# Retention stage of a two-block transformer kernel: x's sums made while a factor is spread, scores scaled in place in PSUM, second root ahead of the keys, last head's gate tiles taken one by one

## The chip, the core and the metric

The kernel runs on one core of a Trainium2 chip. The metric is the device time of one execution in microseconds; the number compared is the median over several runs. Engines: PE (TensorE, matrix products; PEld is its weight load), DVE (VectorE), ACT (ScalarE), POOL (GpSimd), SP (SyncE, which here only issues DMAs). Each engine has its own instruction list, worked through in order; semaphores tie the lists together.

## What is computed

Two blocks over 512 positions of 1024 features, all in fp32. The first block is a convolution mixer and a gated FFN. The second has a retention layer, an MLP, a chunked attention layer and another MLP. The change touches the retention layer only:

```python
def _retention(h, w_in, gn_g, w_out):            # B=1, S=512, 4 heads, dk=256, dv=512, chunks of 64
    q, k, v, g = jnp.split(h @ w_in, [RET_QK, 2 * RET_QK, 2 * RET_QK + RET_VW], axis=-1)
    q = _rope(q, pos)                            # [t1*cos - t2*sin, t1*sin + t2*cos]
    k = _rope(k, pos) * (RET_DK ** -0.5)
    ...
    scores = einsum('bhid,bhjd->bhij', qb, kb) * intra_decay   # and a running state between chunks
    ...                                          # o: decayed (q k^T) v over all earlier chunks and the own one
    mu, var = mean(o), mean((o - mu)**2)         # per position and head
    o = ((o - mu) * rsqrt(var + EPS)) * gn_g
    return (silu(g) * o) @ w_out
```

Here `h = rmsnorm(x) * mix_norm_g`, and x itself is first normalised once more, since this layer sits behind the final norm of the first block. So two factors per position are needed: `rc` (both norms together) for the layer's input and `rc2` (the first norm alone) for the residual x.

## The kernel before

**Precision.** Every fp32 matrix is split into a high half (rounded to the PE's fp32r format) and a low half (the rest), and each product is three matmuls: high by high, low by high, high by low (`product`, lines 865 to 869). For weights, ACT makes the high half (L1420) and POOL the low half (L833), in halves of a block of 128 x 2048. For activations ACT makes the high half and DVE the low one.

**Units.** PE works in units of 24 products of 128 x 512 (three matmuls for each of 8 tiles, or 4 x 2). `unit_done` counts units that PE has ended, `unit_taken` those whose PSUM bank has been read. PSUM has 8 banks (`ps[:, 0..7]`); weights have two slots, so ACT converts the block after next once PE has let go of a slot (`after_unit` waits for a unit and then calls `convert`).

**Retention, its start.** PE runs four units of the first head's queries (units 0, 1, in banks 0, 1) and keys (units 2, 3, in banks 2, 3). Between them it sums the squares (`stats`, bank 4) and spreads the factor `rc` over the partitions by products of ones with `diagonals` (`spread`, L954, bank 5). DVE copies the spread factor to `r_bc` (L2491), multiplies it into the tables cos and sin (L2495) and rotates (`rope`, L2498): four products of a bank with a table into `sg` in SBUF (L2502 to L2505), a subtraction and an addition within `sg` (L2507, L2508). ACT makes the high half of the result (L1438) and DVE the low one (L2515).

**Retention, value and gate.** Each head has seven quarters of a Strassen-like scheme (`HEAD_QUARTERS`: h11, d1, h22, d2, d3, h21, d4), two units each. The quarters d1, h22, d2 and d3 multiply sums of x over tiles and positions. DVE makes these once, at the start (`position_sum`, L2544, four instructions per sum; `w` is an intermediate held in banks 6 and 7), ACT and DVE split them (L1776, L2552), and SP stores three of them in DRAM for the later heads (L637) and fetches them again (L610). The matching sums of weights are made by DMAs of POOL that add onto a loaded block (`add_to`, L785); p1 to p4 are those behind d1 to d4: p3, for instance, is issued when h22's low half is made, and d3 can be converted only when p3 has landed.

**Retention, one head.** Order on PE: h11; for head 0 a second `spread`, of `rc2`, for later heads the scores; d1, h22; for head 0 the scores; d2, d3, mix of tiles 0 and 1, h21, mix of tiles 2 and 3, d4, then (but for the last head) the next head's query units, the 16 transposes of the gated output (`head_turn`, L1204), the next key units, and four output units. h11 writes banks 0 and 1 and waits until the units there are taken; d1 writes banks 2 and 3 and waits until the keys are taken. Scores come in four tiles of 512, 384, 256 and 128 columns in banks 4 to 7. DVE multiplies each with the decay into `ptf` in SBUF (`score`, L2567), ACT makes the high half from `ptf` (L1438) and DVE the low half (`score_lo`, L2558). d3 waits for `value_sum` (L2585), which stands behind the four `score_lo` and two copies on DVE.

**End of a head.** `mixed_stats` gives the variance, ACT the root (`make_root`, L1429), DVE refines it (`refine_root`) into `t4`. The gate's four tiles come from h21 (0 and 1, `gate_sum`) and d4 (2 and 3, `gate_copy`, L2602). ACT applies silu (`gate_curve`, L1711) and then `t4` (`scale_gate`, L1718), DVE forms the gated output (`gated`, L2615), PE turns it. On ACT the order is: silu of 0 and 1, root, the conversions behind the two units of d4, silu of 2 and 3, the four scalings.

**Order.** Nothing is scheduled: each engine's order is the order of its code, and within `ret` that is `head` and the lines behind it.

## Time and profile before

| | us |
|---|---|
| median of 3 runs (lowest, highest) | 1893.45 (1893.13, 1895.30) |
| the profiled execution, its own time | 1893.47 |
| its span, first to last instruction | 1891.5 |
| PE busy in it | 1831.4 (97%) |
| DVE, POOL, ACT busy | 1191.0, 1021.6, 884.3 |
| mean granted TensorE clock | 0.989 |
| retention stage in it | about 536 to 976 |

The profile is of one execution. Times in its rows run from the start of the span. "Idle before" is an engine's time without work ahead of an instruction, put down to the wait that ended last. PE is busy nearly all the time, so the kernel's time changes where PE waits, where its clock is low, or where its work changes.

### The profile page before, as it was taken

How to read it: one execution, taken by the hardware profiler on the slowest of the kernel's cores; microseconds unless marked ns; L12 is line 12 of the kernel's file. 1: busy time of each engine (PE TensorE's matmuls, PEld its weight loads, DVE VectorE, ACT ScalarE, POOL GpSimd, SP SyncE). 2: the span in 40 equal slices, each digit the busy share in tenths (PEclk: the TensorE clock that was granted, in tenths of full speed). 3: DMA queues.
4: the chain of work that ended last, by engine and by line, in shares of the span. 5: the costliest groups of instructions: out<-in, count | busy, mean ns of one | idle time of the engine just before them, and what ended most of it. 6: DMA issues, size and time to landing. Idle time of an engine off the chain costs nothing.

```text
span 1891.5 us, 23910 instructions
## 1 busy us (share of the span) xinstructions
PE 1831.4 (97%) x9348; PEld 1557.3 (82%) x9348; DVE 1191.0 (63%) x1859; ACT 884.3 (47%) x1370; POOL 1021.6 (54%) x447
## 2 busy tenths in 40 slices
PE   9999999999986999999799999999999999999998
PEld 7778889898874888878689898988888887888886
DVE  6986875775776564545466354457877766454546
ACT  5345443342443535252545444455566646353444
POOL 5573465475536456565537575664233336664755
PEclk9999999999998999999899999999999999999999
DMA  5222424432257547473442332312433222414221
GB/s 184 90 89 70 154 67 145 148 108 93 87 178 192 169 115 225 112 208 90 124 156 88 113 112 68 134 45 66 122 111 110 81 79 98 156 53 147 91 89 56
DMA packets 150705, 218.61 MB, mean 116 GB/s; under 512 B 4513, under 2 KB 94897, under 8 KB 150081
## 3 DMA queue, kind: packets, MB, share of 16 engines
q1 hardware_dynamic: 134880, 187.97, 29.9%
q0 software_dynamic: 8448, 16.78, 5.1%
q10 hardware_dynamic: 7264, 12.34, 2.2%
q8 instruction: 74, 1.21, 0.3%
q14 instruction: 39, 0.31, 0.0%
HBM read 207.59 MB, written 9.48 MB: 115 GB/s over the span
## 4 chain that ended last, share of the span: by engine, by line
PE 73%; DVE 10%; ACT 4%; POOL 4%; issue 2%; DMA 2%; ACTq 0%; DVEq 0%
PE ps L867 24%; PE ps L868 23%; PE ps L869 23%; POOL w_lo L833 4%; DMA work<-in_ret_w_in_dram 2%; ACT w_hi L1420 1%; DVE ps L2344 1%; DVE diagonals L2012 1%; PE ps L1204 0%; DVE xl L2038 0%; DVE probs_t_lo L2558 0%; ACT work L1892 0%; DVE probs_t_lo L2787 0%; PE ps L1294 0%; DVE work L2781 0%
## 5 line engine op out<-in xcount | busy, mean ns | idle before, releaser
L833 POOL TENSOR_TENSOR w_lo<-raw,w_hi 128x1024 fp32r<-128x1024 f32 x220 | 532.6, 2430 | 615.1 <-ACT w_hi L1420 615.1
L867 PE MATMUL ps<-xh,w_hi 128*128 128x512 f32 x1280 | 504.2, 394 | 5.1 <-DVE xl L2038 3.0
L869 PE MATMUL ps<-xh,w_lo 128*128 128x512 f32 x1280 | 498.5, 389 | 0.0
L868 PE MATMUL ps<-xl,w_hi 128*128 128x512 f32 x1280 | 498.3, 389 | 0.0
L1420 ACT ACTIVATE w_hi<-raw 128x1024 fp32r<-128x1024 f32 x238 | 247.6, 1057 | 385.1 <-PE ps L869 342.7
L867 PEld LDWEIGHTS ps<-xh,w_hi 128*128 128x128 f32 x1280 | 240.3, 188 | 59.8 <-issue 8.2
L868 PEld LDWEIGHTS ps<-xl,w_hi 128*128 128x128 f32 x1280 | 240.4, 188 | 50.3 <-issue 1.9
L869 PEld LDWEIGHTS ps<-xh,w_lo 128*128 128x128 f32 x1280 | 240.3, 188 | 50.4
L867 PE MATMUL ps<-hid,w_hi 128*128 128x256 f32 (+1 forms) x688 | 228.9, 333 | 2.2 <-DVE att_v L2741 0.9
L868 PE MATMUL ps<-hid,w_hi 128*128 128x256 f32 (+1 forms) x688 | 227.3, 330 | 0.0
L869 PE MATMUL ps<-hid,w_lo 128*128 128x256 f32 (+1 forms) x688 | 227.3, 330 | 0.0
L833 POOL TENSOR_TENSOR w_lo<-work,w_hi 128x1024 fp32r<-128x1024 f32 x60 | 145.3, 2463 | 41.6 <-ACT w_hi L1420 41.6
L867 PEld LDWEIGHTS ps<-hid,w_hi 128*128 128x128 f32 x688 | 131.1, 191 | 15.6 <-issue 2.3
L833 POOL TENSOR_TENSOR w_lo<-down,w_hi 128x1024 fp32r<-128x1024 f32 x40 | 96.2, 2420 | 83.9 <-ACT w_hi L1420 83.8
L869 PEld LDWEIGHTS ps<-hid,w_lo 128*128 128x128 f32 x688 | 130.9, 190 | 12.2
L868 PEld LDWEIGHTS ps<-hid,w_hi 128*128 128x128 f32 x688 | 131.1, 191 | 11.7 <-issue 0.2
L867 PE MATMUL ps<-w_hi,hid 128*128 128x512 f32 x224 | 90.7, 405 | 18.3 <-DVE ps L2585 12.0
L2253 DVE TENSOR_TENSOR x<-x,ps 128x512 f32<-128x512 f32 x84 | 56.9, 684 | 74.8 <-PE ps L869 74.7
L1420 ACT ACTIVATE w_hi<-work 128x1024 fp32r<-128x1024 f32 x60 | 62.0, 1056 | 85.2 <-PE ps L869 43.8
L2702 DVE SCALAR_TENSOR_TENSOR work<-ps,r_bc 128x512 f32<-128x512 f32 x64 | 43.6, 690 | 79.6 <-PE ps L869 79.5
L833 POOL TENSOR_TENSOR w_lo<-holder,w_hi 128x1024 fp32r<-128x1024 f32 x24 | 57.7, 2420 | 59.4 <-ACT w_hi L1420 59.4
L868 PE MATMUL ps<-w_lo,hid 128*128 128x512 f32 x224 | 88.6, 395 | 0.0
(292 smaller groups left out, 3523.1 us busy)
## 6 DMA issues: line engine op xcount, KB each, us to landing
raw<-in_mlp_w_dram SPq DMA_DIRECT2D x40, 1024.0 KB, 5.5
work<-in_mlp_w_dram SPq DMA_DIRECT2D x16, 1024.0 KB, 5.9
raw<-in_ret_w_in_dram SPq DMA_DIRECT2D x12, 1024.0 KB, 5.4
raw<-in_att_w_in_dram SPq DMA_DIRECT2D x12, 1024.0 KB, 5.3
raw<-in_w_gate_dram SPq DMA_DIRECT2D x11, 1024.0 KB, 5.3
raw<-in_w_up_dram SPq DMA_DIRECT2D x11, 1024.0 KB, 5.4
raw<-in_w_in_dram SPq DMA_DIRECT2D x9, 1024.0 KB, 5.1
down<-in_mlp_w_dram SPq DMA_DIRECT2D x8, 1024.0 KB, 5.7
```

What stands on the lines that cost most here:

```text
L833: nc.gpsimd.tensor_tensor(half_of(wl[:, b % 2, :], b, half), half_of(source, b, half), half_of(wh[:, b % 2, :], b, half).bitcast(F32), ALU ...
L867: nc.tensor.matmul(o, a[0], b[0], start=first, stop=False, skip_group_check=True)
L868: nc.tensor.matmul(o, a[0], b[1], start=False, stop=False, skip_group_check=True)
L869: return nc.tensor.matmul(o, a[1], b[0], start=False, stop=last, skip_group_check=True)
L1420: nc.scalar.activation(half_of(wh[:, b % 2, :], b, half), source, ACT.Copy).then_inc(w_hi, c.made(w_hi))
L2012: V.reciprocal(rough, root_rows).then_inc(dve_step, c.made(dve_step))
L2253: V.tensor_tensor(tiles, tiles, ps[:, where, :].rearrange("p (m c) -> p m c", m=2), ALU.add).then_inc(unit_taken, c.made(unit_taken))
L2344: V.scalar_tensor_tensor(total if last else acc, src, w, acc, ALU.mult, ALU.add).then_inc(signal, c.made(signal))
L2702: V.scalar_tensor_tensor(hval[:, u % 2, :], bank(), 0.0, r_bc[:, :], ALU.max, ALU.mult).then_inc(unit_taken, c.made(unit_taken))
```

## The change

Four edits of the retention stage, plus one in SP's queue that goes with them. The number of matmuls does not change.

1. At the start, DVE makes the sums `w` and `d2` between writing the diagonals and reading the spread factor, then takes the factor, rotates the queries, and makes `d1`. ACT converts h11's weights ahead of the halves of the sums, not behind them. `rope` is split: its two products with cos are written in place in PSUM, the subtraction and addition read PSUM and write `sg`, and only the last of these six instructions releases the banks (it was the fourth). The low half is `rope_lo`.
2. The second root is asked for behind d2's low half, `rc2`'s diagonals stand ahead of the rotation of the keys, and the sum `d3` and its halves behind it. PE's scores wait for all four sums' low halves.
3. `score` multiplies in place in PSUM, and both halves are made from there.
4. At the end of a head the root stands between silu of tile 0 and of tile 1. In the last head the scalings of tiles 0, 1, 2 stand ahead of silu of tile 3, and the two conversions of weights behind all of them.
5. SP fetches the next head's query weights right ahead of its key weights, behind d3's conversion; they were fetched behind h11's.

```diff
@@ SP, per head
-                        if more:
-                            converted("h11", h)
-                            fetch("q", h + 1)
                         multiplied("d1", h)
...
                         if more:
                             converted("d3", h)
+                            fetch("q", h + 1)
                             fetch("k", h + 1)
@@ PE, head_scores
                         pe.wait_ge(qk_ready, c.next(qk_ready, 2))
+                        pe.wait_ge(sum_lo, len(SUM_ROW))
@@ ACT
-                            hi_of(pth[:, cut], ptf[:, cut])
+                            hi_of(pth[:, BY_KEY[j]:BY_KEY[j] + n], ps[:, 4 + j, 0:n])
...
                         gate_curve(h, 0)
+                        make_root()
                         gate_curve(h, 1)
-                        make_root()
...
+                        else:
+                            unit_ended()
+                            gate_curve(h, 2)
+                            scale_gate(h, (0, 1, 2))
+                            unit_ended()
+                            gate_curve(h, 3)
+                            scale_gate(h, (3,))
+                            convert(2)
                         turned_hi(h)
...
                     make_root()
                     scale_far(4)
+                    after_unit()
+                    after_unit()
+                    rotated_hi(qh, "q", 0)
                     position_sum_hi("d1")
                     position_sum_hi("d2")
-                    qk_hi_of(qh)
+                    after_unit()
+                    after_unit()
+                    make_root()
                     position_sum_hi("h22")
                     act.wait_ge(sum_lo, SUM_ROW["d2"] + 1)
                     scale_far(0)
+                    rotated_hi(kh, "k", 0)
                     position_sum_hi("d3")
-                    make_root()
-                    qk_hi_of(kh)
@@ DVE
+                    def rope(bank):
...
                         V.tensor_tensor(sg[:, 1, :], a, sin, ALU.mult)
+                        V.tensor_tensor(sg[:, 0, :], b, sin, ALU.mult)
+                        V.tensor_tensor(a, a, cos, ALU.mult)
+                        V.tensor_tensor(b, b, cos, ALU.mult)
+                        V.tensor_tensor(sg[:, 0, :], a, sg[:, 0, :], ALU.subtract)
+                        V.tensor_tensor(sg[:, 1, :], b, sg[:, 1, :], ALU.add).then_inc(unit_taken, c.made(unit_taken, 2))
...
-                        V.tensor_tensor(ptl[:, cut], ptf[:, cut], pth[:, cut].bitcast(F32), ALU.subtract)
+                        V.tensor_tensor(ptl[:, cut], ps[:, 4 + j, 0:SEQ - P * j], pth[:, cut].bitcast(F32), ALU.subtract)
...
-                        V.tensor_tensor(ptf[:, cut], ps[:, 4 + j, 0:n], decay[:, h % 2, 0:n], ALU.mult)
+                        V.tensor_tensor(ps[:, 4 + j, 0:n], ps[:, 4 + j, 0:n], decay[:, h % 2, 0:n], ALU.mult)
```

Two places show how the lists move. The first is DVE's list at the start of the stage, from the second factor's root to the first query or key rotation behind it. `cols` are the small per-position columns, `diagonals` the matrix that PE spreads, `hid` the halves of a sum, `work` the SBUF area of tables, `sg` and sums. Before:

```order
L2691 COPY cols<-cols 128x4
L2523 RECIPROCAL ps<-cols 128x4 [waits curve_made]
L2525 TENSOR_TENSOR cols<-ps,cols 128x4 [waits dve_step]
L2527 SCALAR_TENSOR_TENSOR cols<-ps,cols 128x4 [waits dve_step]
L2529 SCALAR_TENSOR_TENSOR cols<-cols,ps 128x4 [waits dve_step]
L2002 TENSOR_TENSOR diagonals<-ident,cols 128x512 [waits root_refined]
L2502 TENSOR_TENSOR work<-ps,work 128x512 [waits unit_done]
L2503 TENSOR_TENSOR work<-ps,work 128x512
L2504 TENSOR_TENSOR work<-ps,work 128x512
L2505 TENSOR_TENSOR work<-ps,work 128x512
L2507 TENSOR_TENSOR work<-work 128x512 [waits unit_taken]
L2508 TENSOR_TENSOR work<-work 128x512
```

The same place after the change:

```order
L2531 RECIPROCAL ps<-cols 128x4 [waits curve_made]
L2533 TENSOR_TENSOR cols<-ps,cols 128x4 [waits dve_step]
L2535 SCALAR_TENSOR_TENSOR cols<-ps,cols 128x4 [waits dve_step]
L2537 SCALAR_TENSOR_TENSOR cols<-cols,ps 128x4 [waits dve_step]
L2019 TENSOR_TENSOR diagonals<-ident,cols 128x512 [waits root_refined]
L2560 TENSOR_TENSOR hid<-work,hid 128x1024 [waits sum_made,sum_hi]
L2512 TENSOR_TENSOR work<-ps,work 128x512 [waits unit_done]
L2513 TENSOR_TENSOR work<-ps,work 128x512
L2514 TENSOR_TENSOR ps<-ps,work 128x512
L2515 TENSOR_TENSOR ps<-ps,work 128x512
L2517 TENSOR_TENSOR work<-ps,work 128x512 [waits dve_step]
L2518 TENSOR_TENSOR work<-ps,work 128x512
```

The sum h22's low half has moved between the diagonals and the rotation of the keys, and the rotation's last two instructions now read PSUM. Before the change, all four sums stood ahead of these rows; after it, `d3`, its four instructions and its two halves, stands behind them.

The second is ACT's list at the end of the last head. `w_hi<-holder` are the conversions of output weights, `cols<-cols` is the root. Before:

```order
L1711 ACTIVATE work<-work,cols 128x512 [waits unit_taken] x2
L1429 ACT_TABLE_LOAD
L1429 ACTIVATE cols<-cols 128x4 [waits to_curve]
L1420 ACTIVATE w_hi<-holder 128x8x128 [waits holder_landed2,unit_done]
L1420 ACTIVATE w_hi<-holder 128x8x128 [waits holder_landed2]
L1711 ACT_TABLE_LOAD
L1711 ACTIVATE work<-work,cols 128x512 [waits unit_taken] x2
L1718 ACTIVATE work<-work,cols 128x512 [waits gate_made,root_refined]
L1718 ACTIVATE work<-work,cols 128x512 [waits gate_made] x3
L1723 ACTIVATE hid<-ps,prm 128x512 [waits turned] x4
```

The same place after the change:

```order
L1712 ACTIVATE work<-work,cols 128x512 [waits unit_taken]
L1431 ACT_TABLE_LOAD
L1431 ACTIVATE cols<-cols 128x4 [waits to_curve]
L1712 ACT_TABLE_LOAD
L1712 ACTIVATE work<-work,cols 128x512 [waits unit_taken]
L1712 ACTIVATE work<-work,cols 128x512 [waits unit_taken,unit_done]
L1719 ACTIVATE work<-work,cols 128x512 [waits gate_made,root_refined]
L1719 ACTIVATE work<-work,cols 128x512 [waits gate_made] x2
L1712 ACTIVATE work<-work,cols 128x512 [waits unit_taken,unit_done]
L1719 ACTIVATE work<-work,cols 128x512 [waits gate_made,root_refined]
L1419 ACTIVATE w_hi<-holder 128x8x128 [waits holder_landed2] x2
L1724 ACTIVATE hid<-ps,prm 128x512 [waits turned] x4
```

The number of table loads is the same; the conversions have moved from ahead of the last two silus to behind the last scaling.

## Rows read from the trace of the kernel before

**Rows 1.** Who waited for whom, PE, 536 to 976: total us, times, longest.

```profile
PE ps L867 <- DVE ps L2585: 12.0, 3, 9.4
```

**Rows 2.** PE in order of time at the stage's start: start, us, idle before.

```profile
562.26 0.79 PE L867 MATMUL ps<-w_hi,xh 128*128 128x512 f32 x1 [4.91 <-DVE work L2505]
...
577.80 2.08 PE L954 MATMUL ps<-diagonals,ones 128*128 128x128 f32 x8 [7.83 <-DVE diagonals L2002]
580.19 0.80 PE L867 MATMUL ps<-w_hi,hid 128*128 128x512 f32 x1 [0.32 <-DVE work L2505]
...
613.58 0.79 PE L867 MATMUL ps<-w_hi,hid 128*128 128x512 f32 x1 [9.37 <-DVE ps L2585]
```

**Rows 3.** Busy time by stretch: us, five engines with instruction counts, PE clock, DMA share, GB/s.

```profile
928.00:942.00 14.00, 5.45 (x22) 4.79 (x21) 6.62 (x9) 9.82 (x13) 4.65 (x2) 0.63 0.00 0
```

**Rows 4.** Chain that ended last, at the third gap's end: start, us, what.

```profile
616.93 0.43 PE ps L868
...
618.03 0.23 PE ps L868
```

**Rows 5.** DVE in order of time at the stage's start.

```profile
549.94 1.29 DVE L2495 TENSOR_TENSOR work<-work,r_bc 128x512 f32<-128x512 f32 x2
551.27 3.36 DVE L2544 SCALAR_TENSOR_TENSOR ps<-x,prm,ps 128x256 f32<-128x256 f32 x8
...
557.45 1.23 DVE L2552 TENSOR_TENSOR hid<-work,hid 128x1024 fp32r<-128x1024 f32 x1 [1.13 <-ACT hid L1776]
...
561.52 0.68 DVE L2505 TENSOR_TENSOR work<-ps,work 128x512 f32<-128x512 f32 x1
562.24 2.35 DVE L2507 TENSOR_TENSOR work<-work 128x512 f32<-128x512 f32 x1
...
602.48 8.99 DVE L2558 TENSOR_TENSOR probs_t_lo<-work,probs_t_hi 128x512 fp32r<-128x512 f32 x4 [3.57 <-ACT probs_t_hi L1438]
```

**Rows 6.** POOL in order of time, the same stretch.

```profile
559.37 4.67 POOL L833 TENSOR_TENSOR w_lo<-raw,w_hi 128x1024 fp32r<-128x1024 f32 x2 [18.33 <-ACT w_hi L1420]
...
590.67 1.30 POOL L785 DMA_DIRECT2D work<-in_ret_w_in_dram  x1 [0.30 <-POOL w_lo L833]
...
601.07 5.16 POOL L833 TENSOR_TENSOR w_lo<-work,w_hi 128x1024 fp32r<-128x1024 f32 x2 [2.30 <-ACT w_hi L1420]
```

**Rows 7.** ACT in order of time, the same stretch.

```profile
599.92 2.01 ACT L1420 ACTIVATE w_hi<-work 128x1024 fp32r<-128x1024 f32 x2 [6.63 <-DMA work<-in_ret_w_in_dram]
601.84 1.53 ACT L1438 ACTIVATE probs_t_hi<-work 128x512 fp32r<-128x512 f32 x4
```

**Rows 8.** ACT in order of time at the end of the last head.

```profile
928.48 2.00 ACT L1420 ACTIVATE w_hi<-holder 128x1024 fp32r<-128x1024 f32 x2 [2.15 <-PE ps L869]
...
931.80 1.33 ACT L1711 ACTIVATE work<-work,cols 128x512 f32<-128x512 f32 x2
933.04 2.54 ACT L1718 ACTIVATE work<-work,cols 128x512 f32<-128x512 f32 x4
```

**Rows 9.** DVE, the same stretch.

```profile
933.77 3.03 DVE L2615 SCALAR_TENSOR_TENSOR work<-work,cols 128x512 f32<-128x512 f32 x4 [4.65 <-ACT work L1718]
```

**Rows 10.** PE, the same stretch.

```profile
936.95 3.65 PE L1204 MATMUL ps<-ident,work 128*128 128x128 f32 x16 [8.55 <-DVE work L2615]
940.25 0.78 PE L867 MATMUL ps<-hid,w_hi 128*128 128x512 f32 x1
```

**Rows 11.** Chain that ended last, heads 0 to 3.

```profile
842.45 1.75 PE ps L1204 x16
...
889.51 10.77 DMA work<-in_ret_w_in_dram
```

**Rows 12.** SP's issues in order of time, head 1.

```profile
712.90 0.37 SPq L606 DMA_DIRECT2D work<-in_ret_w_in_dram  x1
```

**Rows 13.** ACT in order of time, head 1.

```profile
724.88 2.01 ACT L1420 ACTIVATE w_hi<-raw 128x1024 fp32r<-128x1024 f32 x2 [4.34 <-PE ps L869]
```

**Rows 14.** DMA issues of the whole run: KB each, median us to landing.

```profile
raw<-in_ret_w_in_dram SPq DMA_DIRECT2D x12, 1024.0 KB, 5.4
```

## What the change should do to the time

> **What bounds the kernel now.** I read the page's busy times first, then the list of who waited for whom on PE in the retention stage, then the three engines in order of time around each of PE's gaps. PE is busy 97% of the span, so the question is where it is not. In 536 to 976 us nearly all its idle time lies in four gaps. Three are at the start of the stage: 4.91 us ahead of h11, 7.83 ahead of the second spread, 9.37 ahead of d3 [rows 2]. One is ahead of the last head's transposes, 8.55 [rows 10]. The waits of the kind that end ahead of d3 sum to 12.0 in three heads, so 2.6 are left for heads 2 and 3 [rows 1]. Each big gap costs more than itself. Behind the third, matmuls start 0.43 us apart and later 0.23 apart [rows 4], that is at 1.2 and then at 2.4 GHz, and the stretch 928 to 942 has a mean clock of 0.63 [rows 3]. From the rows I put the slow matmuls behind the first gap at 2.0 us of loss (ten at 0.2), behind the second at 3.4 with the spread's 2.08 where about 0.9 is its due, behind the third at 1.9. With small gaps of 0.3 to 0.7 each around d1 and h22, PE loses about 31 us between the end of the key units (557.35 = 562.26 - 4.91) and d3. The check: h11, spread, d1, h22, scores and d2 at full clock are 4 x 5.45 + 0.9 + 3.75 = 26.5 us (24 products at 0.227, scores 10 tiles of products by width), so d3 could start at 583.8; it starts at 613.58 and then still loses the 1.9.
>
> Why DVE is late there: an instruction with both inputs in SBUF stands still while POOL works. L2507 takes 2.35 where POOL's pair runs from 559.37 for 4.67, and the four-instruction group L2558 takes 8.99 beside POOL's 5.16 and the pair behind it; L2505, which reads PSUM during the same POOL pair as L2507, takes 0.68 [rows 5, 6].
>
> **The change, step by step.** All times are my estimates on the profile's clock, built from its durations. A DVE instruction of 512 columns goes at 0.6 to 0.7 us, a sum's four at 0.42 each (3.36 for eight), a half of 1024 columns 1.23, on ACT 1.06 [rows 5].
>
> *First gap.* `w` and `d2` now lie under the wait for the spread (diagonals end 545.2, spread ends 549.2; the sums' 3.36 fit). Factor copy, tables 1.29, then the rotation. ACT converts h11 at about 545.4, so POOL's 4.67 lie over the tables, two-SBUF instructions: their cost is 1.29 (POOL idle) to 3.6 (a stall like L2507's); I take 2.7, since POOL's pair would end near 551.2. The rotation runs 552.6 to 556.4, six instructions now before the banks are free where four did. That is before PE ends the keys at 557.35. Gap 4.91 becomes 0 and the clock stays up: h11 runs 557.4 to 562.8.
>
> *Second gap.* DVE: d1 to 558.1, q's low half to 559.4, d1's and d2's low halves to 561.8, sum h22 to 563.7, root refined 564.5, then the diagonals. POOL is at d1's weights then (ACT converts them 560.2 to 562.1 behind d2's high half; POOL 561.3 to 566.0). The diagonals read ident and columns, both in SBUF. Cost 0.69 to 2.35, the same two rows as bounds; I take the upper one, since the rotation's subtraction is the same form beside the same POOL work, so they are done at 566.8. PE idles 4.0 us. The spread needs about 1 us, but d1 waits for the keys' banks: h22's low half to 568.1, rotation 3.75, so 571.9. The old wait was released by the fourth instruction; the two more cost 1.3 us here. PE idles 3 us more, the clock is low as behind the other gaps of this kind, and I charge 1.9 + 1.2. d1 ends at 579.3 (before: near 587.4).
>
> The Trainium skill, page "SBUF — State Buffer", section "SBUF: two separate sides", says that a two-SBUF-input VectorE instruction and a GpSimd one take a port pair as an exclusive lock and the loser blocks fully. It speaks for edit 3 and against the moved tables and diagonals: by it these stall 1.4 and 1.5 us; with the rows' lower bounds instead, d3 would start some 1.5 us earlier and the time be 1867.5.
>
> *Third gap.* DVE behind the rotation: d3 to 573.6, k's low half to 574.8, d3's to 576.1, factor copy and the kept products of h11. ACT reaches h22's conversion at 574.7, POOL ends it at 580.5, and h22 runs on PE 579.3 to 584.8 with no wait over 0.7. Scores end at 588.5, d2 at 594.0. The new bound is the transfer p3: POOL issues it behind h22's low half, at 580.8. Before, it was issued at 590.67 and ACT went on at 599.92 [rows 6, 7], 9.25 later; in head 3 the like transfer took 10.77 [rows 11]. The fetch of sum d3 (multiplied d1 at 579.3, stored by 581.5) now runs beside it as in head 3, so I take 10.3 and 591.1. ACT then converts d3, 2.0, and makes the scores' high halves, 1.53 [rows 7]. DVE's low halves follow each within 0.7 (PSUM input, no stall): 595.6. Two copies and `value_sum`, 2.0: d3 starts at 597.6. Gap 3.6 instead of 9.37. I take it without a clock loss, as its length is below all four that had one. Gain of the three together: 613.58 + 1.9 - 597.6 = **17.9**.
>
> *Last head.* The last unit ends at 928.4. Before: conversions 2.00, table load 1.3 (930.48 to 931.80), silus, scalings to 935.58, DVE to 936.8 [rows 8, 9]. Now ACT has silu of 0 at 924.2, table load, root 925.6, load 926.9, silus of 1 and 2 by 928.3, three scalings of 0.63 by 930.1, silu 930.8, last scaling 931.4. DVE's last of four follows at 932.2. PE starts turning 4.7 earlier. The conversions now lie in front of ACT's reading of the turned tiles: they end at 933.4, so the first product comes at 934.9 where it came at 940.25 [rows 10]. That is 5.35. If the clock stays up (3.8 us of idle) 0.8 more is saved on the first products: **6.1**. If it falls, the transposes take 3.65 and not 1.75 [rows 10, 11] and the gain is 4.6.
>
> *Heads 1 to 3.* PE waits only 2.6 + some 0.7s there [rows 1], for the chain through p3, which is bound by the transfer and not by DVE. I give it 0.4. The score halves' stalls vanish from DVE but no one waits for them. Root ahead of silu: nothing. The later release of the key banks lies under the first output unit, 5.45 long. The later fetch of the next queries goes out at 712.90 with the keys' [rows 12]; 1 MB lands 5.4 later [rows 14], ACT takes it at 724.88 [rows 13], so 6 us are in hand: nothing.
>
> *Sum.* 17.9 + 6.1 + 0.4 = 24.4 off the profiled execution's own 1893.47 gives 1869.1; the median shown is 1893.45, the same. I say 1869.
>
> **Rivals.**
> (A) *The new bound bites harder.* p3 lands 11.5 after issue, d3 starts 1.2 later, PE's gap is 4.8 and the clock falls as behind the 4.91 one (+2), and it falls in the last head too (+1.5): 1869.1 + 4.7 = 1874. For it: the 4.91 gap is the nearest, and two other gaps of mine are near 4. Against: the third needs two things at once.
> (B) *The stalls do not come.* Tables and diagonals find POOL between its instructions, p3 takes 9.25, the clock stays up ahead of d1: 1.5 + 1.0 + 1.9 less, 1865.
> (C) *The change doesn't do what it says.* Score halves from PSUM stall as those from SBUF did: 8.99 instead of 3, d3 6 us later and a slow clock behind, 1869.1 + 8 = 1877. Against: L2505's 0.68 beside POOL.
> (D) *Slower.* The next queries, now queued with the keys behind d3, come late in heads 0, 1, 2. ACT wants them 12 us after issue; with POOL's pair and PE ready near 735, PE itself is held only from 18.6 after issue. To eat 24.4 us it must be 8.1 late in each of three heads, landing 27 after issue; at 30 it is 3 x 11.4 - 24.4 = +9.8, 1903. Against: 5.4 median, no row near it.
>
> **How the numbers follow.** Forecast 0.52, A 0.19, B 0.15, C 0.10, D 0.02, the rest (0.02) anything else near no change. The forecast's own spread is the bounds used: tables and diagonals, transfer 9.25 to 11.5, the last head's clock: about 1866.5 to 1871.5. To hold 8 in 10 the range takes in A and most of B: 1864 to 1875.5. What a measurement of this kernel tells from no change is about 0.2%, 3.8 us. Faster 0.96, same 0.02, slower 0.02.
>
> **What would show each step.** PE without a gap ahead of h11; spread near 567 and d1 near 572; L2507's successor at 0.7 and not 2.3; tables near 2.7; p3's landing as releaser of d3's conversion and value_sum ahead of d3 near 597.6; score low halves at 0.3 to 0.7 each; transposes near 932 on the old clock with PE's clock still full. I would be wrong if PE had a new gap in the middle of head 0, or ahead of the first output units, where turned tiles now wait for ACT's conversions.

## The result, and the profile after

The changed kernel took 1877.5 us (median of four executions, 1875.3 to 1877.67), the kernel before 1893.44 beside it: a ratio of 0.9911 with a 95% interval of 0.9894 to 0.9928. The forecast was 1869 with a range of 1864 to 1875.5. So the sign and most of the steps came out, and the size did not: 16 us were gained of 24.4. Four more executions of the same kernel, run later beside the experiments, gave 1873.75, 1873.82, 1875.37 and 1878.16. The eight have a median of 1876.4. The profiled execution of after is the one of 1877.67, its span 1875.7.

I count gains as the start of the same matmul in the profile of before minus its start in that of after. The first view is PE in order of time, start and duration in us and the idle time ahead; it answers [rows 2].

```profile
566.33 2.07 PE L952 MATMUL ps<-diagonals,ones 128*128 128x128 f32 x8 [3.75 <-DVE diagonals L2019]
571.19 0.79 PE L865 MATMUL ps<-w_hi,hid 128*128 128x512 f32 x1 [2.79 <-DVE work L2518]
```
```profile
598.91 0.80 PE L865 MATMUL ps<-w_hi,hid 128*128 128x512 f32 x1 [5.15 <-DVE ps L2592]
599.50 0.63 PE L866 MATMUL ps<-w_lo,hid 128*128 128x512 f32 x1
...
602.86 0.39 PE L865 MATMUL ps<-w_hi,hid 128*128 128x512 f32 x1
```

There is no gap ahead of h11 any more. The spread starts 11.5 us earlier, d1 9.0, d3 14.7 (613.58 - 598.91). The gap of 5.15 ahead of d3 is what is left of 9.37, and the matmuls behind it still take 0.63 until 602.5.

The list of who waited for whom on PE, 536 to 976, in total us, times and the longest, answers [rows 1]:

```profile
PE ps L865 <- DVE ps L2592: 8.7, 4, 5.1
PE ps L1203 <- DVE work L2622: 4.9, 2, 4.2
PE ps L952 <- DVE diagonals L2019: 3.8, 1, 3.8
PE ps L865 <- DVE work L2518: 2.8, 1, 2.8
```

DVE in order of time in the prologue answers [rows 5]. The tables took 2.74. The low halves of the scores take 1.69 from PSUM where they took 8.99 from SBUF. The copy of four columns in the middle is new to this list, and so are the diagonals' 0.69 behind it:

```profile
549.73 2.74 DVE L2699 TENSOR_TENSOR work<-work,r_bc 128x512 f32<-128x512 f32 x2
...
561.34 1.97 DVE L2706 COPY cols<-cols 128x4 f32<-128x4 f32 x1
...
565.58 0.69 DVE L2019 TENSOR_TENSOR diagonals<-ident,cols 128x512 f32<-128x512 f32 x1
...
595.11 1.69 DVE L2566 TENSOR_TENSOR probs_t_lo<-ps,probs_t_hi 128x512 fp32r<-128x512 f32 x4 [6.64 <-ACT probs_t_hi L1440]
```

POOL's issue of the transfer p3 and of p4, SP's fetch of the sum for d3, and ACT's conversion of d3 that p3 releases, each from its own engine's list in order of time. They answer [rows 6, 7]:

```profile
579.86 1.30 POOL L783 DMA_DIRECT2D work<-in_ret_w_in_dram  x1 [0.30 <-POOL w_lo L831]
...
586.22 1.29 POOL L783 DMA_DIRECT2D holder<-in_ret_w_in_dram  x1 [0.30 <-POOL w_lo L831]
```
```profile
579.96 0.58 SPq L610 DMA_DIRECT2D hid<-position_sums  x1
```
```profile
592.59 2.01 ACT L1419 ACTIVATE w_hi<-work 128x1024 fp32r<-128x1024 f32 x2 [12.55 <-DMA work<-in_ret_w_in_dram]
594.50 1.40 ACT L1440 ACTIVATE probs_t_hi<-ps 128x512 fp32r<-128x512 f32 x4
```

The end of the last head on ACT and PE answers [rows 8, 10]. The order is as forecast, and PE's idle time is 4.17 instead of 8.55, but the 16 transposes still take 3.05, where they took 1.75 in head 2 [rows 11]:

```profile
915.29 1.93 ACT L1719 ACTIVATE work<-work,cols 128x512 f32<-128x512 f32 x3
917.12 0.70 ACT L1712 ACTIVATE work<-work,cols 128x512 f32<-128x512 f32 x1
917.92 0.72 ACT L1719 ACTIVATE work<-work,cols 128x512 f32<-128x512 f32 x1
918.55 1.99 ACT L1419 ACTIVATE w_hi<-holder 128x1024 fp32r<-128x1024 f32 x2
```
```profile
919.57 3.05 PE L1203 MATMUL ps<-ident,work 128*128 128x128 f32 x16 [4.17 <-DVE work L2622]
922.27 0.78 PE L865 MATMUL ps<-hid,w_hi 128*128 128x512 f32 x1
```

Followed along the whole program, the gain is 14.7 at d3 of head 0, 13.0 when the last head's last unit ends, 18.1 behind that head's end, 15.7 behind 1320 us of the changed kernel, and 15.8 at the end. The drop of 2.4 lies in the attention layer, where the change touches nothing. The questions were therefore: why d3 is 1.3 us later than forecast and slow behind; what is lost in heads 0 and 1; whether the last head's clock is PE's standing still; and what the 2.4 are.

### The profile page after: what moved, and what is told of

Its sections match the earlier page's. It is cut to its first block, busy times and chain, and to the rows that moved or that the text cites. A ratio compares the mean times of both kernels' runs of the same rounds, so it can differ in the third digit from the quotient of the medians.

```text
span 1875.7 us, 23906 instructions
## 1 busy us (share of the span) xinstructions
PE 1830.6 (98%) x9348; PEld 1557.2 (83%) x9348; DVE 1168.3 (62%) x1859; ACT 883.9 (47%) x1370; POOL 1019.2 (54%) x447
## 4 chain that ended last, share of the span: by engine, by line
PE 72%; DVE 10%; ACT 4%; POOL 4%; DMA 2%; issue 2%; ACTq 0%; DVEq 0%
PE ps L865 23%; PE ps L867 23%; PE ps L866 23%; POOL w_lo L831 4%; DMA work<-in_ret_w_in_dram 2%; ACT w_hi L1419 1%; DVE ps L2361 1%; DVE diagonals L2029 1%; DVE probs_t_lo L2810 0%; PE ps L1203 0%; DVE xl L2055 0%; DVE work L2804 0%; ACT work L1909 0%; PE ps L1293 0%; DVE work L2622 0%
## 5 line engine op out<-in xcount | busy, mean ns | idle before, releaser
L865 PE MATMUL ps<-w_hi,hid 128*128 128x512 f32 x224 | 90.5, 404 | 15.9 <-DVE ps L2592 8.7
L867 PE MATMUL ps<-w_hi,hid 128*128 128x512 f32 x224 | 88.6, 396 | 0.0
```

The lines of the kernel that those rows point to most:

```text
L865: nc.tensor.matmul(o, a[0], b[0], start=first, stop=False, skip_group_check=True)
L867: return nc.tensor.matmul(o, a[1], b[0], start=False, stop=last, skip_group_check=True)
```

## The experiments

All times stand beside runs of the kernel before on the same chip; its medians in the five groups were 1893.83 (e1 to e4), 1892.97 (e5 to e8), 1893.93 (e9 to e11, the changed kernel again), 1894.28 (e12 to e14) and 1894.15 (e15 to e17). Variants of the changed kernel whose medians are one or two us apart mostly have overlapping intervals of their ratios. There a reading rests on the traces at the place of the edit, one trace for each kernel, and not on the medians.

### One part alone

**The scores alone.** The kernel before, with part 3 of the change only.

```diff
-                            hi_of(pth[:, cut], ptf[:, cut])
+                            hi_of(pth[:, BY_KEY[j]:BY_KEY[j] + n], ps[:, 4 + j, 0:n])
...
-                        V.tensor_tensor(ptl[:, cut], ptf[:, cut], pth[:, cut].bitcast(F32), ALU.subtract)
+                        V.tensor_tensor(ptl[:, cut], ps[:, 4 + j, 0:SEQ - P * j], pth[:, cut].bitcast(F32), ALU.subtract)
...
-                        V.tensor_tensor(ptf[:, cut], ps[:, 4 + j, 0:n], decay[:, h % 2, 0:n], ALU.mult)
+                        V.tensor_tensor(ps[:, 4 + j, 0:n], ps[:, 4 + j, 0:n], decay[:, h % 2, 0:n], ALU.mult)
```

> The kernel before with one edit of the change alone: scores scaled in place in PSUM, the high and low halves read from there. In the kernel before the four low halves took 8.99 us (602.48 to 611.5) beside POOL; from PSUM they took 1.69 in the changed kernel. Theory (the SBUF read is what stalls, and in the kernel before it stands alone behind the transfer p3): the low halves end near 604.9, two copies and value_sum follow, d3 starts near 607 where it was 613.58, and with the gap of 9.37 down to about 3 the clock may stay up: 6.5 to 8.4 us saved, 1885 to 1887. Rival (something else, such as POOL's low half of d3's weights, sets d3's start): under 3 us saved, above 1890.

Measured: 1884.86 (1884.14 to 1887.29), ratio 0.9957 (0.9944 to 0.9969). PE at d3:

```profile
605.96 0.50 PE L867 MATMUL ps<-w_hi,hid 128*128 128x512 f32 x1 [1.63 <-DVE ps L2584]
606.29 0.40 PE L868 MATMUL ps<-w_lo,hid 128*128 128x512 f32 x1
```

The theory holds; the gain is at or just above its upper end of 8.4 (9.0 by the medians, 8.1 by the ratio). The gap is 1.63, the clock stays up, and 9.5 us are gained by 620, of which the trace keeps 7.9. This one part alone was worth about half of what the whole change brought.

**The scores back in SBUF**, all else of the change kept (the same lines the other way round).

> The changed kernel with the scaled scores written to SBUF as before and halved from there; all else of the change stays. Theory (stall behind the late p3): low halves take 6 to 9 us again beside POOL's low halves of d3, d3 starts 5 to 7 us later than 598.9, and the time is 1883 to 1885. Rival (with the prologue earlier DVE no longer meets POOL there): within 2 us of the changed kernel, 1876 to 1879.

Measured: 1886.64 (1883.51 to 1887.37), ratio 0.9956 (0.9943 to 0.997). DVE in order of time:

```profile
595.21 8.93 DVE L2566 TENSOR_TENSOR probs_t_lo<-work,probs_t_hi 128x512 fp32r<-128x512 f32 x4 [7.05 <-ACT probs_t_hi L1440]
```

d3 starts at 606.25, 7.3 later than in the changed kernel, with ACT's conversion at the same 592.65. The time is above the 1883 to 1885 that I expected: 8.4 us are lost by 650, and this trace has the loss in the attention layer too (below). The forecast's reason for part 3 is shown from both sides, and its rival C, that the halves stall from PSUM too, is out.

**The last head alone.** The kernel before, with the last head's part only.

```diff
...
+                        else:
+                            make_root()
+                            gate_curve(h, 1)
+                            unit_ended()
+                            gate_curve(h, 2)
+                            scale_gate(h, (0, 1, 2))
+                            unit_ended()
+                            gate_curve(h, 3)
+                            scale_gate(h, (3,))
+                            convert(2)
```

> The kernel before with the last head's part of the change alone (second root between the first two silus, gate tiles scaled as they come, the two conversions behind them); heads 0 to 2 keep their order. The changed kernel gained 4.9 us at this place, with a clock that still fell ahead of the transposes. Theory (places are independent): 4 to 5 us saved, 1888.5 to 1889.5, transposes again at 3.0 us or more. Rival (the loss against the forecast's 6.1 came from the other edits): 6 us or more, below 1887.5.

Measured: 1890.21 (1888.55 to 1892.18), ratio 0.9981 (0.9973 to 0.999). That is 3.6 saved and less than the 4 to 5 expected. The trace shows why: it gains 4.4 at this place and loses 1.0 at d3 of head 1, where nothing is changed against the kernel before. That loss matters for the reading of heads 0 to 3 below.

### Why d3 starts late

**ACT's order.** In head 0 ACT makes the scores' high halves ahead of d3's conversion.

```diff
-                        after_unit()
-                        after_unit()
-                        if h == 0:
-                            scores_hi(range(ST))
+                        if h:
+                            after_unit()
+                            after_unit()
+                        else:
+                            unit_ended()
+                            unit_ended()
+                            scores_hi(range(ST))
+                            convert(2)
```

> The changed kernel, but in head 0 ACT makes the four high halves of the scores ahead of d3's weights, which wait for p3. In the changed kernel ACT stood 12.55 us at p3, and the scores, scaled at 588.5, were halved only behind it: low halves 595.1 to 596.8, value_sum ended 599.5, d3 598.9. Theory (ACT's order is half of the third gap): only p3's landing (592.6), ACT's first half and POOL's first low half are left, d3 starts near 596.3, PE's gap is about 2.5, and the clock stays up: 2.5 to 4.5 us saved, 1873 to 1875. Rival (POOL's low half or the transfer alone sets the start): under 1 us saved, 1876.5 to 1877.5.

Measured: 1873.7 (1872.52 to 1877.37), ratio 0.9898 (0.9885 to 0.9912). PE at d3, and ACT:

```profile
596.48 0.77 PE L865 MATMUL ps<-w_hi,hid 128*128 128x512 f32 x1 [2.58 <-issue]
597.04 0.63 PE L866 MATMUL ps<-w_lo,hid 128*128 128x512 f32 x1
```
```profile
592.88 2.01 ACT L1419 ACTIVATE w_hi<-work 128x1024 fp32r<-128x1024 f32 x2 [3.95 <-DMA work<-in_ret_w_in_dram]
```

d3 starts where expected, 2.4 us earlier. Yet the clock does not stay up: the next five matmuls take 0.63. A gap of 2.58 has the slow matmuls behind it here, and one of 1.63 in the kernel with the scores alone has none. The median is within the 1873 to 1875 that I expected.

**The fetch of the sum held back** until p3 has landed, as a measure of p3 by itself.

```diff
+                            sp.wait_ge(p3_landed, 16)
                         fetch_sum("d3")
```

> The changed kernel, but in head 0 SP fetches the sum for d3 only when p3 has landed; in the changed kernel both 1 MB transfers went out at 579.9 and p3 landed 12.6 us after its issue (9.1 in the kernel before, where the fetch went out 3.1 us ahead of it). Theory (they share the engines): p3 lands 9 to 10 us after issue, near 589.5, and d3 waits for its sum instead. Rival (p3 is slowed by the other accumulating transfer, p4, issued at 586.2 on the same queue): p3 still takes over 12 us. The time itself is no measure here, as the sum then comes later than d3 wants it: 1876 to 1880.

Measured: one execution, 1877.26. ACT and SP:

```profile
588.65 2.01 ACT L1420 ACTIVATE w_hi<-work 128x1024 fp32r<-128x1024 f32 x2 [7.74 <-DMA work<-in_ret_w_in_dram]
```
```profile
588.62 0.58 SPq L610 DMA_DIRECT2D hid<-position_sums  x1
```

p3 now lands 8.7 us after its issue at 579.89, not 12.6. It is the sum's fetch that delayed it. How it did so, the DMA view of the changed kernel shows for 579 to 586 (queue, packets, MB, share of 16 engines), and for the held one for 579 to 585:

```profile
q1 hardware_dynamic: 279, 1.06, 53.3%
q0 software_dynamic: 47, 0.10, 8.2%
```
```profile
q0 software_dynamic: 233, 0.48, 55.1%
q1 hardware_dynamic: 12, 0.01, 0.6%
```

q1 carries SP's fetch, q0 POOL's accumulating transfers. With both issued at the same moment, the fetch moved its whole megabyte and p3 moved 47 packets in the seven microseconds; without it p3 was at 233 one microsecond earlier. POOL was at d2's low halves (580.68, 5.24 us, and 580.71, 5.25) in both, so its own work is not what kept p3 back.

What the fetch costs p3 is a late start more than a shared way. Alone, p3's first packets go 2.0 us after its issue. Up to 585 the changed kernel's view has 233 packets of the fetch and none of p3. Its first goes at 585.2, 5.3 us after the issue, when the fetch is nearly through, and from there p3 needs about 7 us, as it does alone. In 12 of the 15 traces in which both are issued together p3 starts at 585.2 to 585.5. In e14 below, where the fetch was issued 0.6 behind p3 and not 0.1, p3's packets started at 581.9, before the fetch's, and between 584 and 587 the two moved 148 and 146 packets; p3 landed after 11.5. Why a fetch that is issued in the same moment holds back p3's start is not shown.

The Trainium skill, page "DMA: Bandwidth & Descriptors", section "Queues, rings and completion order", says that each engine takes packets in turn from the queues that have work. The 148 to 146 of e14 are such turns. The 279 to 47 here are not; that page alone would have let me expect about half of the packets for p3.

**The next queries fetched at their old place.**

```diff
+                        if more:
+                            converted("h11", h)
+                            fetch("q", h + 1)
...
                             converted("d3", h)
-                            fetch("q", h + 1)
```

> The changed kernel with the next head's queries fetched as before, behind h11's low half, and not with the keys behind d3's. Theory (the forecast's: the fetch is hidden at either place): within 1 us of the changed kernel, 1876.5 to 1878.5. Rival (at its old place it runs into p2 and p3, which now go out early): p3 lands later than 12.6 us after issue, d3 starts up to 2 us later, 1878 to 1880.

Measured: 1879.26 (1876.87 to 1879.36), ratio 0.9923 (0.9908 to 0.9938). The rival holds. p3 is issued at 580.16, and two fetches stand beside it:

```profile
594.57 2.00 ACT L1420 ACTIVATE w_hi<-work 128x1024 fp32r<-128x1024 f32 x2 [14.49 <-DMA work<-in_ret_w_in_dram]
```

So from issue to conversion p3 takes 8.8 us alone, 12.7 with one fetch and 14.4 with two. Here the queues of POOL and SP (q0 and q1), once p3 has started, do go in turn, from 587 to 594:

```profile
q0 software_dynamic: 529, 1.05, 81.0%
q1 hardware_dynamic: 534, 0.55, 28.8%
```

The queries' fetch is no winner there: it takes 20.5 us to land. Part 5, which the forecast priced at nothing, is worth 2.0 us at d3 (600.88 against 598.91), since the earlier prologue has put p3 where the old fetch would run; in the kernel before that fetch went out at 576.49, took 7.9 us and was through before p3's issue at 590.67. The 2.0 is one trace against one, and the ratios of the two kernels overlap.

**p4 held back** until p3 has landed (`pool.wait_ge(p3_landed, ...)` ahead of p4's issue), on top of ACT's order above and the root's old place below; first in all heads, then in head 0 alone. The comparison is the same kernel without it.

> The changed kernel with both changes of order that have helped singly: scores' high halves ahead of d3's conversion in head 0, root behind both silus in heads 0 to 2. Singly they gave 1873.7 and 1875.0. Theory (different places, their gains add: 2.4 and 0.9 in the traces): 1872 to 1873.5. Rival (what the root's place gives is taken back at the next transfer): 1873.5 or more.

Measured: 1872.13 (1869.3 to 1874.07), ratio 0.9883 (0.9868 to 0.9898). That is within the 1872 to 1873.5 that the theory of two adding gains gave; its trace gains 20.7 in all.

> The changed kernel with the scores' high halves ahead of d3's conversion in head 0, the root behind both silus in heads 0 to 2, and in all heads POOL issues the transfer p4 only when p3 has landed (POOL is idle there). Theory (p3 shares the engines with whatever runs beside it: 8.7 us with the sum's fetch held back, 12.7 with it, 14.4 with the queries' fetch as well): without p4's first 6 us p3 lands up to 1 us earlier in each head, d3 starts near 595.5 in head 0, and PE's waits of 0.9 to 1.6 ahead of d3 in heads 1 to 3 shrink: 1 to 3 us faster than the same kernel with p4 at its old place. Rival (p4 waits behind p3 on their queue anyway and takes nothing from it): no difference.

Measured: 1874.66 (1874.09 to 1878.18), slower than the 1872.13 beside it and not 1 to 3 faster. p3 landed 1.5 us earlier than in the trace beside it in head 0. In heads 1 to 3 its trace loses 5.2 us between 700 and 900 on the time axis of the kernel before, where the one beside it loses 1.3. Part of that is the clock: d3 of head 1 has slow matmuls behind a gap of 1.84. What the later p4 costs by itself is not separated.

> The changed kernel with the scores' high halves ahead of d3's conversion in head 0, the root behind both silus in heads 0 to 2, and in head 0 alone p4 issued only when p3 has landed. With p4 held in all heads the trace stood 1.5 us better behind head 0 and lost 2.3 and 1.9 us at d3 and d4 of heads 1 and 2, where the same kernel with p4 at its old place lost 1.2 and 0. Theory (in head 0 p3 shares with p4, elsewhere the later p4 makes something late): p3 lands near 591.8, d3 near 595.9, 1 to 1.6 us saved against the kernel with the two changes of order, 1870.5 to 1871.5. Rival (head 0's gain is chance): 1872 or more, p3 again at 592.6.

Measured: 1873.53 (1872.57 to 1874.45); ACT's conversion of d3 begins at 593.02, where it began at 593.27 without. The rival holds: nothing is gained, and the early landing of e9 (591.76), with the same hold on p4, did not come again. Over the traces with p3 and this one fetch together ACT's conversion begins 11.5 to 13.4 us after p3's issue, mostly 12.5 to 13.

**Sum and p4 both held back** in head 0.

```diff
+                            sp.wait_ge(p3_landed, 16)
                         fetch_sum("d3")
...
-                if kind == "d2":
+                if kind == "d2" and head_of(b) or kind == "d3" and head_of(b) == 0:
                     pool.wait_ge(w_lo, lows[2 * b + 2])
                     add_to("b12", "b21", head_of(b), p4_landed)
```

> The same two changes of order, and in head 0 the sum for d3 is fetched when p3 has landed and p4 issued behind d3's low halves. Theory: p3 lands near 588.2, the sum 5.5 to 6 us later near 594, weights ready by 592, so d3 starts at 594 with PE's gap near 0.7: 2 us faster than with both at their old places. Rival (p4, now landing near 603, makes d4's weights late): PE gets a wait ahead of d4 and the gain is gone.

Measured: 1878.4 (1877.31 to 1878.47). d3 starts at 593.89, with all of the third gap gone, and then:

```profile
608.80 2.00 ACT L1420 ACTIVATE w_hi<-holder 128x1024 fp32r<-128x1024 f32 x2 [12.65 <-DMA holder<-in_ret_w_in_dram]
```
```profile
612.88 0.79 PE L866 MATMUL ps<-hid,probs_t_hi 128*128 128x512 f32 x1 [5.83 <-DVE hid L2609]
```

p4, issued at 595.01 between the fetches of queries (594.74) and keys (595.17), takes 13.8 us to ACT's conversion and holds ACT. ACT's values behind it, and so PE, come late, and the clock falls again. On the time axis of the kernel before, a gain of 21.7 at 620 is down to 11.5 at 650. The rival holds: the order that frees one transfer starves the next.

### The copy that waits

The copy of four columns placed behind the queries' rotation, where POOL is idle.

```diff
                     rope(0)
+                    V.tensor_copy(ms, r1c).then_inc(to_curve, c.made(to_curve))
                     position_sum("d1")
...
                     position_sum_lo("d2")
-                    V.tensor_copy(ms, r1c).then_inc(to_curve, c.made(to_curve))
```

> The changed kernel with the copy of four columns for the second root made right behind the queries' rotation, where POOL is idle (551.3 to 560.9), and not at 561.34 beside POOL's low half of d1, where it took 1.97 us against 0.16. Theory (the copy waits for POOL's instruction, and DVE's chain to the second spread and to the keys' banks is critical): copy 0.16, spread and d1 1.8 us earlier, second gap 1.8 us shorter in all, p3 issued as much earlier: 1.5 to 2 us saved, 1875.5. Rival (the sum that follows, with two SBUF inputs, then waits for POOL in its place): under 0.5 us saved, 1877.

Measured: 1877.91 (1876.48 to 1879.05). DVE:

```profile
556.36 0.16 DVE L2702 COPY cols<-cols 128x4 f32<-128x4 f32 x1
...
563.90 2.44 DVE L2019 TENSOR_TENSOR diagonals<-ident,cols 128x512 f32<-128x512 f32 x1
```

The rival holds, with another instruction than I named. The copy is back at 0.16, the sum is not slowed, and the diagonals, two inputs in SBUF, now come while POOL is still busy and take 2.44 where they took 0.69. The spread starts at 566.40 instead of 566.33. POOL's two halves end at 563.29 and 565.59 in the changed kernel and at 563.50 and 565.80 here. The copy ended at 563.31 there, the diagonals end at 566.34 here: each waited for the half that it met, and the stall passes from one of DVE's instructions to the next. The Trainium skill, page "SBUF — State Buffer", section "SBUF: two separate sides", states the exclusive lock also for copies in a two-port mode; the 1.97 against 0.16 for a copy of 128x4 agrees.

### The root's place in heads 0 to 2

Root back behind both silus there, the last head as changed.

```diff
                         gate_curve(h, 0)
-                        make_root()
-                        gate_curve(h, 1)
+                        if more:
+                            gate_curve(h, 1)
+                            make_root()
+                        else:
+                            make_root()
+                            gate_curve(h, 1)
```

> The changed kernel with the second root of heads 0 to 2 back behind both first silus, as in the kernel before; the last head stays as changed. In the changed kernel the four gating steps of heads 0 and 1 took 6.9 us (3.15 in the kernel before), since ACT's scaled tiles come 1.3 us earlier and DVE now meets POOL's pair, and PE waits 0.7 to 1 us ahead of the transposes. Theory (the earlier root costs by that meeting): gating 3.2 again in heads 0 and 1, that wait gone, 0.7 to 1.8 us saved, 1875.5 to 1877. Rival (the root's place is free and the wait comes from something else): no change, 1877.5.

Measured: 1874.97 (1874.57 to 1877.17), ratio 0.9906 (0.989 to 0.9923). The four gating steps on DVE in head 0, changed kernel and then this one:

```profile
628.70 6.89 DVE L2622 SCALAR_TENSOR_TENSOR work<-work,cols 128x512 f32<-128x512 f32 x4 [3.83 <-ACT work L1719]
```
```profile
629.55 3.16 DVE L2626 SCALAR_TENSOR_TENSOR work<-work,cols 128x512 f32<-128x512 f32 x4 [4.62 <-ACT work L1719]
```

POOL in order of time, again the changed kernel and then this one:

```profile
625.96 4.77 POOL L831 TENSOR_TENSOR w_lo<-work,w_hi 128x1024 fp32r<-128x1024 f32 x2 [6.03 <-ACT w_hi L1419]
...
631.55 2.82 POOL L831 TENSOR_TENSOR w_lo<-raw,w_hi 128x1024 fp32r<-128x1024 f32 x1
```
```profile
625.39 4.79 POOL L831 TENSOR_TENSOR w_lo<-work,w_hi 128x1024 fp32r<-128x1024 f32 x2 [5.45 <-ACT w_hi L1419]
...
632.40 2.57 POOL L831 TENSOR_TENSOR w_lo<-raw,w_hi 128x1024 fp32r<-128x1024 f32 x1 [1.02 <-ACT w_hi L1419]
```

In the changed kernel the gating starts 0.9 earlier, meets the end of POOL's pair and then its next half, and is done at 635.6. With the root back it falls between the two and is done at 632.7. PE's 0.7 ahead of head 0's transposes is gone, 0.9 us in the trace. The ratios, 0.9906 here and 0.9911 and 0.9901 in the changed kernel's two sets of executions, tell nothing of so little.

### The clock, and the attention layer

**The changed kernel again**, four more executions and another profile.

> The changed kernel as it is, more executions beside the others. In its profile 2.4 us were lost at 1315 us in the attention layer, where the change touches nothing, to a lower clock; four of the other traces do not show that drop. Theory (the drop falls in some executions and not in others): two groups of times about 2 us apart, near 1875.4 and 1877.6. Rival (it belongs to this kernel): one group near 1877.5.

Measured: 1873.75, 1873.82, 1875.37 and 1878.16 (median 1874.6). Busy time by stretch, 1310 to 1325 (us, five engines with instruction counts, PE's granted clock, DMA share, GB/s), first execution and then this one:

```profile
1310.00:1325.00 15.00, 13.04 (x92) 12.63 (x92) 8.66 (x21) 6.32 (x15) 1.80 (x1) 0.89 0.62 170
```
```profile
1310.00:1325.00 15.00, 13.21 (x104) 12.62 (x104) 10.59 (x30) 8.40 (x17) 2.64 (x2) 1.00 0.62 169
```

One execution had the lower clock there and the other had not. What PE did before it shows in the same matmul of the two, the changed kernel's first trace and then this one:

```profile
1315.53 0.30 PE L1275 MATMUL ps<-k_parts,q_hi 128*128 128x128 f32 x1 [1.96 <-DVE att_v L2764]
```
```profile
1314.88 0.30 PE L1275 MATMUL ps<-k_parts,q_hi 128*128 128x128 f32 x1 [1.43 <-DMA k_odd<-k_odd]
```

PE stood still for 1.96 us in the one and 1.43 in the other, and for 1.07 in the kernel before. In four more of the traces (e3, e8, e14, e17) it stood for 1.68 to 2.22, the clock fell behind it, and 2.1 to 2.6 us were lost. In all the rest it stood for at most 1.49 and the clock stayed up: they lose 0.4 at most, and three with a filled last head (e13, e15, e16), where that gap was 0.2 or less, gain 0.9 to 1.1. So the same kernel shows the loss in one execution and not in the other, and it goes with the length of a gap that varies; why the gap varies is not shown.

**Filling the gaps.** Small products of ones with ones, 128x128 in fp32, into a bank that nobody reads, on top of the two changes of order (e13 and e14 also hold p4 once, as above).

```diff
+                        else:
+                            pe.wait_ge(unit_taken, 2 * head_block("h11", h) + 12)
+                            keep_warm(24, 3)
                         head_turn()
...
                         if h == 0:
+                            keep_warm(24, 4)
                             spread()
+                            keep_warm(16, 4)
```

> The kernel just described plus, in the last head, 24 small products (128x128, fp32, into a bank that nobody reads) between d4 and the transposes, where PE stands still for 4.17 us and the clock then reads low: 16 transposes take 3.64 us and the first products start 0.43 apart. Theory (the clock falls because PE stands still): with PE at work the transposes take 1.75 and the first products start 0.23 apart, 2 us saved or somewhat more. Rival (the clock falls anyway there, or the small products overrun the gap at 0.2 us each): no gain or up to 1 us lost.

> As before, plus 24 and 16 of the same small products in head 0 ahead of the second spread and ahead of d1, where PE stands still for 3.8 and 2.9 us and d1's first twelve matmuls then start 0.43 apart. Theory (that slow clock delays the units that free h22's weight slot, so p3 goes out late): d1 at full clock, p3 issued about 2 us earlier, d3 up to 2 us earlier. Rival (d3 waits for p3 and the stored sum, both of which hang on DVE and not on PE): under 0.5 us saved.

Measured: 1870.96 (1869.27 to 1874.33) and 1871.15 (1869.62 to 1872.04), against 1873.53 without. The products overran the gaps: 24 of them, 48 entries in the trace, took 5.5 us, and at the last head's end the trace of e13 gains 0.8 more than that of e12, not the 2 expected. In e14 d1 ran at full clock, and p3 was issued at the same 579.86 as in the changed kernel, so the theory that the slow clock delays p3's issue is out. So I shortened them: 16 in the last head alone, then 16 and 11 more in head 0, beside the kernel with none.

> The changed kernel with the two changes of order (scores' high halves first in head 0, root behind both silus in heads 0 to 2) and 16 small products in the last head's gap. At 0.23 us each, as 48 halves of them took 5.5, they fill 3.7 of its 4.17 us. Theory (the clock alone): transposes at their old start, 1.9 instead of 3.64 us long, first product 2.3 to 2.8 us earlier than without them: 1869.5 to 1870.5. Rival (another cause makes the transposes slow): as without them.

> As before, and 16 and 11 of the small products ahead of the second spread and of d1 in head 0 (gaps of 3.77 and 2.89 us). Theory (p3's issue hangs on DVE, and PE catches up before d3): d1 at full clock, yet p3 again issued near 579.9 and d3 where it was, no gain over the kernel with the last gap filled alone. Rival (the slow clock is on the path): 1 to 2 us faster than that one.

> The same kernel with the two changes of order and no small products, beside the other two: it had 1872.1 median with a spread of 1869.3 to 1874.1. Theory: 1872 to 1873, one or two of five executions 2 us off the rest for the landing of p3 and the clock in the attention layer. Rival (the fill's gain was chance): equal to the filled ones.

Measured: 1869.39 (1867.87 to 1869.7), 1867.92 (1867.34 to 1869.49) and 1872.41 (1871.07 to 1874.39); ratios to the kernel before 0.9868 (0.9851 to 0.9884), 0.9863 (0.9849 to 0.9878), 0.9886 (0.9872 to 0.9901). The last head on PE, without (e11) and with (e15):

```profile
916.30 3.64 PE L1203 MATMUL ps<-ident,work 128*128 128x128 f32 x16 [4.17 <-DVE work L2630]
919.59 0.77 PE L865 MATMUL ps<-hid,w_hi 128*128 128x512 f32 x1
```
```profile
910.92 3.73 PE L959 MATMUL ps<-ones 128*128 128x128 f32 x32
915.25 1.94 PE L1203 MATMUL ps<-ident,work 128*128 128x128 f32 x16 [0.61 <-DVE work L2633]
```

With PE at work in the gap the transposes take 1.94 instead of 3.64. From the end of the last unit to the output units the filled traces of e15 and e16 gain 5.9 each, those of e11 and e17 4.3 and 4.6. So the slow clock there comes of PE's standing still, and it is worth about 1.4. The first product comes only 1.8 earlier (917.79 against 919.59) and not the 2.3 to 2.8 that I expected, since PE now waits 0.61 for the gated output and 0.59 for POOL's low half ahead of it. The medians of e15 and e17 are 3.0 apart and their traces 5.1; of the 5.1 the attention layer makes 3.0, where e17's trace lost 2.1 and e15's gained 0.9.

In the prologue the fill left p3's issue at 580.0 once a start of the whole program 1.9 later is taken off (581.92). In the two traces with that fill, p3 released ACT at 591.4 and (less the 1.9) at 591.7; of the others with the fetch beside it only e9, 591.8, was below 592.4. With the 1.9 taken off, e16's trace stands 1.4 ahead of e15's behind d3, about what the medians show. But the executions of the two overlap: whether the second fill brings anything, and how it would act on p3, stays open.

## Why the prediction was right or wrong, step by step

**First gap: right.** No gap ahead of h11, which started at 556.98 (forecast 557.4). Tables 2.74 (2.7), rotation 552.50 to 556.3 (552.6 to 556.4).

**Second gap: right in sum.** Spread at 566.33 (forecast 566.8) and d1 at 571.19 (571.9). The stall came on the copy of four columns and not on the diagonals. That the diagonals still ended near the forecast was in part luck: they could not end much before POOL's pair (565.59), as e8 shows, and the copy's stall happened to take up just that time. The forecast gave their stall as 1.5; its own rows give 2.35 - 0.69 = 1.7, which changes no sum. The slow clock behind it was as charged, and e14 shows that p3's issue does not hang on it.

**Third gap: here the sum failed.** p3 was issued at 579.86 (580.8 forecast), nearly 1 early. Its landing was sized at 10.3 between 9.25 and 11.5, and measured 12.6 to 12.7, above both ends. I took the rows of the kernel before and of head 3 as bounds. In neither did the two transfers go out together. In the kernel before the fetch of the sum was 3.1 us ahead of p3:

```profile
587.54 0.58 SPq L610 DMA_DIRECT2D hid<-position_sums  x1
```

In head 3 it was 2.1 behind (891.58 against 889.51). I read the new case as that of head 3; it was one of its own, since both go out within 0.1 us and p3 starts only when the fetch is nearly through. e6, the changed kernel and e7 show its price: 8.7, 12.6 and 14.3 from issue to landing. Behind it, ACT's conversion and the scores' halves took what I said, but a gap of 5.15 has the slow matmuls behind it, which I left out. The reason that I gave, a gap shorter than all four that had cost clock, did not hold: ahead of d3 gaps of 2.40 to 2.58 (e17, e11, e15, e4), all shorter than the 3.6 forecast, had slow matmuls behind them too. Together: 14.7 by d3 and no more afterwards, instead of 17.9. That is 3.2 of the missing 8.6. In kind it is rival A, which had 0.19, with the transfer 1.1 us worse still.

**What I did not ask:** ACT's order there. I counted conversion and halves one behind the other on the path, correctly, and did not see that the halves had been ready to make since 588.5. e4 takes 2.4 off d3's start by that alone.

**Heads 0 to 3: wrong sign.** Forecast +0.4, measured -1.7 (14.7 to 13.0). "Root ahead of silu: nothing" failed: 0.9 in head 0, shown by e5. About 1 more is lost at d3 of head 1, but e2 loses the same 1.0 there with nothing changed ahead of it: the profile of before had a good execution at that point. I took one execution's 2.6 us of waits [rows 1] as the kernel's.

**Part 5: wrong the other way.** Priced at nothing, worth 2.0 at d3 once the prologue is early (e7). It did not show as a gain against my sum because I had left the collision out on both sides.

**Last head: mechanism right, size off by the clock.** 4.4 at the first transpose and 5.1 behind the first products, against 4.7 and 6.1. The transposes came at 919.57; on the time axis of before and with the 13.0 gained by then that is 932.6, against 932.2. I had let the clock stay up over 3.8 us; it fell. The fills show its price, about 1.4, near the 1.5 that I gave it, and the filled traces gain 5.9 here, near the 6.1.

**The attention layer: not in the sum.** 2.4 lost by a lower clock that some executions have, behind a gap that is longer in them. Of the eight executions of the changed kernel four lie between 1873.75 and 1875.37 and four between 1877.41 and 1878.16. The forecast's range held the first four. One of each group was profiled, and this loss is 2.1 of the 2.3 between them; whether it makes the two groups is not shown for the others. The three executions of before that I had, 1893.13 to 1895.3, already showed 2 us between them, and I let them widen nothing.

In all the misses are 3.2 (prologue) + 2.1 (heads 0 to 3) + 1.0 (last head) + 2.4 (attention layer) = 8.7, and 24.4 less 8.7 is 15.7, against the trace's own 15.8.

The kernel with the lowest median is the changed one with the scores' halves first, the root back in heads 0 to 2 and the gaps filled: 1867.92, 1.4% under the kernel before and 0.5% under the change.

## What to carry to other kernels

When a change makes a transfer start earlier, list every other transfer that will now start in the same microseconds, and do not size it by the same transfer at its old place. DVE's stalls beside POOL ended here with POOL's instruction, so moving one small instruction out of the way passed the stall to the next one; what removed it was another form, here the operand in PSUM (8.99 to 1.69 us), or a place between POOL's instructions (6.89 to 3.16). And where an engine waits for a late transfer, look at what stands behind that wait and was ready long before.

## What the runs showed of the hardware

An accumulating transfer of 1 MB issued by POOL landed after 8.7 us alone: its first packets went 2.0 us after the issue, and under way it moved about 205 GB/s. With a plain fetch of 1 MB issued at the same moment it landed after 12.6: in 13 of 15 traces its first packet went only 5.2 to 5.6 us after the issue, when the fetch was nearly through. With two fetches it took 14.3. Once both queues were under way they took turns (529 packets and 534 in e7, 148 and 146 in e14).

A copy of 128x4 in SBUF took 1.97 us beside a POOL instruction and 0.16 without. Filling a gap of PE of 4.17 us with products that nobody reads brought 16 transposes from 3.64 to 1.94 us. Behind gaps of PE of 2.58, 4.17 and 5.15 us the clock read low, and behind one of 1.63 it did not. The length of the gap alone does not settle it: the clock fell behind gaps of 1.68 (e17, attention layer) and 1.84 (e9, head 1), and stayed up behind 1.82 (e13, head 2), 2.01 (e10, head 0) and 2.26 (e14, ahead of d3). And two executions of one kernel differed by 2.3 us, 2.1 of it through the clock and the gap at a single point.
